# A hybrid decoder step on one core: one barrier per stage, first w_out slices and result rows split in the dilated stage, and a new order of the projection's first tiles and its last

## What is computed

```python
def _project(xn, pos, w_in, g_q_a, w_q_b, g_kv_a):
    z = xn @ w_in
    ...
    cq = _rmsnorm(z[..., :o1], g_q_a)
    q = (cq @ w_q_b).reshape(B, S, MLA_HEADS, MLA_NOPE + MLA_ROPE)
    ...
    ckv = _rmsnorm(z[..., o1:o2], g_kv_a)
    kr = _rope(z[..., o2:o3][:, :, None, :], pos)[:, :, 0, :]
    dq = _rope(z[..., o3:o3 + dw].reshape(B, S, DIL_HEADS, HEAD_DIM), pos)
    dk = _rope(z[..., o3 + dw:o3 + 2 * dw].reshape(B, S, DIL_HEADS, HEAD_DIM), pos)
    dv = z[..., o3 + 2 * dw:].reshape(B, S, DIL_HEADS, HEAD_DIM)
```

## Time and profile before

| | us |
|---|---|
| median of 3 runs | 1820.08 (1819.71 to 1823.69) |
| the profiled execution | 1819.3 |
| its span in the profile | 1817.7 |
| PE busy, share of the span | 1734.8, 95% |
| TensorE's mean granted clock, of full speed | 0.975 |

### The profile page before, as it was taken

One profiled execution on the slowest core, in us unless ns is written; L12 is line 12 of the kernel. 1 busy time (PEld: TensorE's weight loads), 2 busy tenths in 40 slices (PEclk: granted clock), 3 DMA queues, 4 the chain that ended last, 5 costly groups with the idle time before them and its releaser, 6 DMA issues.

```text
span 1817.7 us, 28003 instructions
## 1 busy us (share of the span) xinstructions
PE 1734.8 (95%) x9955; PEld 1511.8 (83%) x9955; DVE 860.7 (47%) x1802; ACT 660.8 (36%) x1329; POOL 573.3 (32%) x533
## 2 busy tenths in 40 slices
PE   7999979999997999999799999999999999999997
PEld 6788868888886888888688989888898898888985
DVE  6433325677775776766443332333423333333235
ACT  5222115666675666675322312111112121121113
POOL 0000003665561767778101312212112122131221
PEclk9999987999998999999899999999999999999999
DMA  8232133232326565655512668496585775956812
GB/s 283 96 105 102 67 106 101 54 102 63 85 61 162 164 179 160 179 159 180 193 50 49 132 144 136 114 164 118 118 161 120 152 115 129 161 110 133 150 43 103
DMA packets 156061, 227.44 MB, mean 125 GB/s; under 512 B 31063, under 2 KB 128984, under 8 KB 149528
## 3 DMA queue, kind: packets, MB, share of 16 engines
q1 hardware_dynamic: 153086, 159.39, 29.6%
q0 software_dynamic: 2880, 66.85, 22.1%
HBM read 201.12 MB, written 91.93 MB: 161 GB/s over the span
## 4 chain that ended last, share of the span: by engine, by line
PE 49%; DVE 1%; DMA 1%; ACT 0%; POOL 0%; issue 0%; ACTq 0%; DVEq 0%
PE wide L2476 22%; PE turn L2498 14%; PE rest L2477 7%; PE wide L2159 5%; DMA out_y_prompt<-f_gc 1%; PE wide L2574 1%; DVE o_wl L2139 1%; PE turn L2171 0%; DVE f_gc L2454 0%; ACT f_gc L2391 0%; PE rest L2483 0%; ACT f_rows L2398 0%; POOL f_st L2322 0%; PE rest L2507 0%; DVE f_al L2442 0%; DVE o_tl L2107 0%
## 5 line engine op out<-in xcount | busy, mean ns | idle before, releaser
L2411 DVE TENSOR_TENSOR acc<-turn,acc 128x512 f32<-128x512 f32 x198 | 136.5, 691 | 205.9 <-PE turn L2498 205.9
L2498 PE MATMUL turn<-f_dh,f_ah 128*128 128x512 f32 x396 | 157.8, 399 | 4.4 <-DVE f_al L2442 4.0
L2279 POOL TENSOR_TENSOR f_gl<-f_graw,f_gh 128x1024 fp32r<-128x1024 f32 x21 | 50.5, 2404 | 350.2 <-ACT f_gh L2329 350.2
L2498 PE MATMUL turn<-f_dl,f_ah 128*128 128x512 f32 x396 | 157.7, 398 | 0.0
L2498 PE MATMUL turn<-f_dh,f_al 128*128 128x512 f32 x396 | 157.6, 398 | 0.0
L990 POOL TENSOR_SCALAR a_pr<-a_pr,a_rden 128x256 f32<-128x256 f32 (+7 forms) x128 | 94.1, 747 | 187.7 <-DVE a_rden L1090 187.6
L2425 DVE SCALAR_TENSOR_TENSOR f_gc<-wide,f_coef,f_gc 128x832 f32<-128x832 f32 x44 | 47.7, 1084 | 209.4 <-ACT f_lasts L2349 206.5
L701 PE MATMUL zp<-win_h,xT_h 128*128 128x512 f32 (+1 forms) x288 | 112.7, 391 | 0.0
L701 PE MATMUL zp<-win_l,xT_h 128*128 128x512 f32 (+1 forms) x288 | 111.5, 387 | 0.0
L701 PE MATMUL zp<-win_h,xT_l 128*128 128x512 f32 (+1 forms) x288 | 111.5, 387 | 0.0
L1031 ACT ACTIVATE a_pr<-a_pr,a_nm 128x256 f32<-128x256 f32 (+7 forms) x128 | 98.6, 772 | 21.5 <-DVE a_nm L1084 20.8
(11 more groups left out here) (365 smaller groups left out, 4658.5 us busy)
## 6 DMA issues: line engine op xcount, KB each, us to landing
out_s_win_k<-in_state_win_k POOLq DMA_DIRECT2D x10, 3264.0 KB, 42.5
out_s_win_v<-in_state_win_v POOLq DMA_DIRECT2D x10, 3264.0 KB, 44.9
acc<-in_state_win_k SPq DMA_DIRECT2D x16, 768.0 KB, 6.0
acc<-in_state_win_v SPq DMA_DIRECT2D x16, 768.0 KB, 5.6
f_uraw<-in_w_up SPq DMA_DIRECT2D x22, 512.0 KB, 4.8
f_draw<-in_w_down SPq DMA_DIRECT2D x11, 1024.0 KB, 33.1
f_graw<-in_w_gate SPq DMA_DIRECT2D x21, 512.0 KB, 8.1
acc<-in_cache_kv_latent SPq DMA_DIRECT2D x128, 64.0 KB, 1.8
```

Of the source, the lines that this page charges most:

```text
L2279: nc.gpsimd.tensor_tensor(w_lo[n][:], w_raw[n][:], w_hi[n][:].bitcast(F32), ALU.subtract)\
L2411: nc.vector.tensor_tensor(a, dp[h][:], a, ALU.add).then_inc(S["d_add"], 1)
L2498: last = nc.tensor.matmul(dp[h][:], a[:, c, t * P:(t + 1) * P], w[:, c, h * 512:(h + 1) * 512], start=(c == 0 and j == 0), stop=(c == 1 an ...
```

## The change

**Barriers.** A class `Semaphores` takes the place of the clears: a stage's semaphores are cleared by POOL at the start of the next stage, and each stage has only its block's barrier. Semaphores that live across a stage are kept to the end. SP no longer waits at the end of the attention for its last stores: the waits are in the output stage, on SP behind the x loads, and on ACT before slice 7 of w_out.

**Early slices.** Three tiles of 2 x 1024 columns (`io["lead"]`) serve first as buffers of the window side. At the end of the dilated stage slices 0 and 1 of w_out are split into them (lead_hi on ACT, lead_lo on POOL), and row tile 0 (lead_rows on ACT and DVE). Later they are buffers of the MLP. On DVE the merge of the last sample (a_qn) is moved ahead of one copy to a_ot. ACT and DVE split only slices 2 to 7 in the output stage. For tile 0 PE takes both column halves of a slice in a row. x rows 0 and 1 are loaded without a wait, x rows 2 to 7 behind the sixth of the low slices, row tile 2 without a wait. Split of tile 1 is ahead of the gate slice on ACT, and a fill of the padding rows goes from DVE's lead to the end of tile 0.

**Project.** In the first two tiles group 2 of t1 comes ahead of the latent transposes of t1, t0's group 3 ahead of t1's query, and t1's group 3 ahead of its key_value; ACT, DVE and SP follow. In the last tile (the samples) group 3 comes ahead of the query, and the latent keys and values, which nobody reads for the samples, are not computed (6 matmuls and two copies).

```diff
             store_dq(t0)
             store_dk(t0)
             turns_in(t0)
+            store_dv(t0)
             store_dq(t1)
             store_q(t1)
-            store_dv(t0)
             store_dk(t1)
             turns_in(t1)
+            store_dv(t1)
             store_kv(t1)
-            store_dv(t1)
             with sp.Fori(0, 2) as it:
...
-                key_turned(t)
-                query(t)
-                sliding_value(t)
-                key_value(t)
+                if samples(t):
+                    sliding_value(t)
+                    query(t)
+                else:
+                    key_turned(t)
+                    query(t)
+                    sliding_value(t)
+                    key_value(t)
...
                 key_value(t0)
                 latent_hi(t1)
                 key_turned(t1)
+                sliding_value(t0)
                 query(t1)
-                sliding_value(t0)
                 prep(Step.of(2))
                 square(Step.of(3))
+                sliding_value(t1)
                 key_value(t1)
-                sliding_value(t1)
 
             walk(act, prep, main, lead)
...
-                query(t)
-                group(t, 3)
-                key_value(t)
+                if samples(t):
+                    group(t, 3)
+                    query(t)
+                else:
+                    query(t)
+                    group(t, 3)
+                    key_value(t)
 
             def lead():
...
                 group(t0, 2)
+                group(t1, 2)
                 latent(t1)
-                group(t1, 2)
+                group(t0, 3)
                 query(t1)
-                group(t0, 3)
                 prep(Step.of(2))
+                group(t1, 3)
                 key_value(t1)
-                group(t1, 3)
...
     def sync_end(self, sp):
-        if self.events is self.stages[1]:
-            for f in range(2):
-                sp.wait_ge(self.S[f"o_out{f}"], 16 * 2 * PAIRS)
...
-    "vector": {(0, "out"): -2, (1, "k_turn"): 1, (1, "score"): 1},
+    "vector": {(1, "lead_rows"): -3, (0, "out"): -2, (1, "k_turn"): 1, (1, "score"): 1},
...
+        elif e[0] == "lead_lo":
+            i = e[1]
+            wh, rows, wl = self.io["lead"]
+            pool.wait_ge(self.io["lead_hi"], i + 1)
+            nc.gpsimd.tensor_tensor(wl[:, i, :], self.io["acc"][:, i, :], wh[:, i, :].bitcast(F32), ALU.subtract)\
+                .then_inc(self.io["lead_lo"], 1)
 
     def scalar(self, act, e):
         S, R, nc = self.S, self.ring.S, self.nc
...
+        if e[0] == "lead_hi":
+            i = e[1]
+            act.wait_ge(self.io["w_ahead"][0], 16)
+            act.wait_ge(S["o_ps"], 3 * DEC_B - 1)
+            nc.scalar.copy(self.io["lead"][0][:, i, :], self.io["acc"][:, i, :]).then_inc(self.io["lead_hi"], 1)
+        elif e[0] == "lead_rows":
+            act.wait_ge(self.io["o_ahead"], 16)
+            act.wait_ge(S["o_ps"], 3 * DEC_B)
+            nc.scalar.copy(self.io["lead"][1][:, 0, :], self.io["acc"][:, PT, :]).then_inc(self.io["lead_hi"], 1)
         bank = self.ring.ready(act, e) if self.bank_use(e) else None
...
-        if e[0] == "pre":
+        if e[0] == "lead_rows":
+            rows = self.io["lead"][1]
+            dve.wait_ge(self.io["lead_hi"], 3)
+            nc.vector.tensor_tensor(rows[:, 1, :], self.io["acc"][:, PT, :], rows[:, 0, :].bitcast(F32), ALU.subtract)\
+                .then_inc(self.io["lead_lo"], 1)
+        elif e[0] == "pre":
...
             x = io["x_prompt"].rearrange("(t p) d -> p t d", p=P)
-            sp.wait_ge(S["w_lo"], 2)
             sp.dma_start(acc[:, 0:2, :], x[:, 0:2]).then_inc(S["x_in"], 16)
-            sp.wait_ge(S["w_lo"], KC)
+            sp.wait_ge(S["w_lo"], KC - 2)
             sp.dma_start(acc[:, 2:PT, :], x[:, 2:PT]).then_inc(S["x_more"], 16)
             ahead["sync_split"](sp)
             sp.dma_start(acc[0:NS, PT, :], io["x_sample"]).then_inc(S["x_last"], 16)
+            for done, n in io["stored"]:
+                sp.wait_ge(done, n)
             with sp.Fori(2, PT) as n:
...
             def lead():
-                split(Step.of(0))
-                for k in range(KC):
+                for k in range(2, KC):
                     act.wait_ge(io["w_ahead"][k // 2], 16)
-                    nc.scalar.copy(wh[:, k, :], acc[:, k, :]).then_inc(S["w_hi"], 1)
+                    if k == KC - 1:
+                        for done, n in io["stored"]:
+                            act.wait_ge(done, n)
+                    nc.scalar.copy(wh[k], acc[:, k, :]).then_inc(S["w_hi"], 1)
+                split(Step.of(1))
                 ahead["scalar"](act)
-                split(Step.of(1))
...
         def tensor(pe):
             def prep(t):
-                pe.wait_ge(S["t_lo"], t.n + 1)
+                if t.first:
+                    pe.wait_ge(io["lead_lo"], 3)
+                else:
+                    pe.wait_ge(S["t_lo"], t.n)
                 if not t.first and not t.second:
 
                     pe.wait_ge(S["h_ok"], t.n - 1)
-                for c in range(2):
+                halves, slices = range(2), range(KC)
+                for c, k in ([(c, k) for k in slices for c in halves] if t.first else [(c, k) for c in halves for k in slices]):
                     cols = slice(c * 512, c * 512 + 512)
-                    for k in range(KC):
-                        if t.first and c == 0:
-                            pe.wait_ge(S["w_lo"], k + 1)
-                        for i, (a, b) in enumerate(((oT_h, wh), (oT_h, wl), (oT_l, wh))):
-                            last = nc.tensor.matmul(mp[t.odd][:, cols], a[t.odd][:, k, :], b[:, k, cols],
-                                                    start=(k == 0 and i == 0), stop=(k == KC - 1 and i == 2))
+                    if t.first and c == 0 and k > 1:
+                        pe.wait_ge(S["w_lo"], k - 1)
+                    for i, (a, b) in enumerate(((oT_h, wh), (oT_h, wl), (oT_l, wh))):
+                        last = nc.tensor.matmul(mp[t.odd][:, cols], a[t.odd][:, k, :], b[k][:, cols],
+                                                start=(k == 0 and i == 0), stop=(k == KC - 1 and i == 2))
...
+            pool.wait_ge(O["t_lo"], 1)
...
+            io["sems"].clear()
...
+    def clear(self):
+        for n in ranges([s.num for s in self.groups[-2][1]]):
+            self.nc.gpsimd.sem_clear(n)
+
+    def close(self):
+        if len(self.groups) > 1:
+            self.groups.pop(0)[0].close()
...
         for phase in PHASES:
-            if phase is attention:
-                io["acc"] = ctx.enter_context(nc.sbuf_tensor("acc", [P, NT, D_MODEL], F32))
-                io["w_ahead"] = [ctx.enter_context(nc.semaphore(f"w_ahead{i}")) for i in range(4)]
-                io["o_ahead"] = ctx.enter_context(nc.semaphore("o_ahead"))
-            with ExitStack() as own:
-                used = []
-
-                def sem(name):
-                    used.append(own.enter_context(nc.semaphore(name)))
-                    return used[-1]
-
-                phase(nc, sem, io)
-
-                for n in ranges([s.num for s in used]):
-                    nc.gpsimd.sem_clear(n)
-                nc.all_engine_barrier()
-
-
+            sems.open()
+            phase(nc, sems.sem, io)
+            sems.close()
```

101 lines of the change are left out of this document (69 added, 32 removed).

## The result

Over eight runs of each, side by side, the changed kernel takes 1804.36 us (1800.69 to 1813.02) and the kernel before 1822.03 (1819.71 to 1823.78): ratio 0.9911, 95% interval 0.9894 to 0.9927. By the ratio that is 16 us (17.7 between the medians), not 9.6. Its profiled execution took 1801.88, span 1800.3, against 1819.3 and 1817.7: 17.4 less of span.

The account below looks back on a forecast made before the run. PE was busy 95% of the span, so only its waits or half clock could be won. Gains 0.8 + 1.3 + 7.6 - 0.1 = 9.6 us gave 1809.7 profiled, 1810.5 for the median; range 1806.5 to 1815.5.

Parts of the forecast that it names:

- The MLP reuses the early buffers, with its waits behind the last output tile: 0: MLP, under other edits: reusing the early slices' buffers there was costed at 0 us.
- Output boundary, the opening: Dilated to output stage: opens at about 876.2, 2.7 us earlier; PE waits 1.1 us in place of 7.4.
- Early slices and rows: End of the dilated stage: work moved ahead of the boundary costs 0, at most 1 us; margin 0.3.
- rival (2): Rows arrive late at the output boundary, or the project gap stays as long: sum 6.0 to 7.0, 1813.5 us, chance 0.12.
- Tile 0: Output stage: PE is never short of slices, so tile 0 ends at 887.2, 9.4 us earlier.
- Tile 2: Output stage: PE waits 1.2 to 2.0 us, taken as 1.7, for row tile 2's load, queued behind 3 MB of x rows.
- The clock: Output stage: a half-clock stretch or the stall for tile 2 takes 1.8 us, leaving 7.6 of 9.4.
- rival (1): Output stage: second loss of clock after a stall of some 2 us for tile 2; boundary 5.8, 1812.3 us, chance 0.22.
- Project stage: First tiles gain 0.8 us (gap 3.6 in place of 4.1, half clock takes 2.2); last tile gains 1.3.
- The range: Whole kernel: 1806.5 to 1815.5 us, from the better case to the second loss of clock.
- (4): Output stage: tile 2's load slower, with the 3 MB taking 26 us; stall 16.3, time 1825.0 us, chance 0.05.

Follow-up runs that it names:

- e7: Changed kernel with fillers placing the lead tiles and f_ah, f_al all at 128 modulo 256, as o_wh and o_wl; 1803.45 us, ratio to before 0.9916.
- e6: Kernel before, with a 160-byte filler ahead of f_ah and f_al, giving them the place of w_down's halves modulo 256; 1810.43 us, ratio 0.9951.
- e12: Changed kernel with the waits for the last stores at the attention's end and a second barrier at two phase boundaries put back; 1806.57 us, ratio to before 0.9933.
- e4: Changed kernel with 32-byte fillers for both the lead tiles and f_ah, f_al, so all start at multiples of 64 bytes; 1810.23 us, ratio to before 0.9939.
- e8: e7 with the rows of the input weights' high half (win_h) also padded from 7808 to 7936 bytes; 1802.2 us, ratio to before 0.9902.
- e11: Changed kernel with output row tile 0 in the old order, all eight slices for the left column half, then the right; 1806.76 us, ratio to before 0.9938.
- e9: e8 with row tile 2 loaded ahead of the 3 MB of x rows and tile 0's rows ahead of w_out's last two loads; 1795.64 us, ratio to before 0.9870.
- e3: Changed kernel with a 32-byte filler beside the lead tiles only, so they start at a multiple of 64 bytes; 1809.78 us, ratio to before 0.9942.
- e10: Changed kernel with every project stage edit taken back (tile orders, six unused matmuls, stores' order); 1806.34 us, ratio to before 0.9928.
- e5: Separate kernel of matmuls only, varying the operands' byte offsets; 48 matmuls took 10.96 us at distance 0 modulo 256, 11.20 to 11.29 elsewhere, 11.05 with moving 64 ahead.

## Why the prediction was wrong, point by point

**The failed step** is "The MLP reuses the early buffers, with its waits behind the last output tile: 0". The waits were looked at, the place was not. The term measured -7.8 us in the MLP (0.80 in each of ten passes). The same reuse has a counterpart in the output projection, where 0.23 a matmul was carried over from before: +1.3 in tiles 3 to 8 and about 0.7 in tiles 0 to 2 (0.4 in tiles 0 and 1 against e7, 0.3 in tile 2 as in the other even tiles). e6 shows the MLP's term alone in the kernel before: 25.29 to 24.49, ratio 0.9951.

**Output boundary, the opening: right.** Forecast 1.1 us from the last a_o matmul to the first of the output stage, measured 1.22, and e12 shows what the old way costs here: 3.1.

**Early slices and rows: right, with the rival in it.** Costed at 0 with 1 as its bound and a margin of 0.3: the margin was 0.3 in the changed kernel's profile, and 1 us was paid in e4, e7, e8 and e11. This was rival (2), in four of the profiles of the changed order.

**Tile 0: right.** No wait on o_wl; tiles 0 and 1 took 22.28 from the opening to the transposes against the forecast 22.0; in e7, with the operands placed alike, 21.89. e11 shows that the order of the halves carries it: without it tile 0 takes 14.4 in place of 11.2.

**Tile 2: size right, and the cause not refuted.** A wait of 1.2 to 2.0 was forecast, 1.48 was measured. It was put down to the 3 MB alone. The chain names the gate slice as well: it took 8.07 us to land where it took 6.8 before, and POOL's split of it holds SP. Whether that cost anything isn't shown. The 3 MB were issued at 880.35; with the 10.9 us that they took before they landed at 891.3 (an estimate, the trace has no landing for them), and tile 2 was cast 3.4 later, where 2.9 was forecast. Tile 2 was usable 8.8 us after its issue at 885.87, and 4.3 us where it went ahead of the 3 MB (e9). The Trainium skill, "DMA: Bandwidth & Descriptors", section "Queues, rings and completion order", has descriptors consumed in ring order; the two traces agree with it.

**The clock: the sum came out, the case was another.** 1.8 were set aside for a lost clock or a stall; here the stall was paid and the clock held. In e4, e7 and e8 (waits of 2.6, 3.0 and 2.2) it was lost after the stall, rival (1); in e3 and e10 (1.97 and 2.19) it held. Forecast for tiles 0 to 2 was 7.6, measured 6.86, and the missing 0.7 is what the placement took there.

**Project stage: right in sum, wrong in its halves.** Forecast 0.8 + 1.3 = 2.1, measured 1.73 in this pair and 2.3 on the means. The gap in the first tiles (timeline) was 3.29, not 3.6:

```profile
55.06 0.80 PE L706 MATMUL zp<-win_h,xT_h 128*128 128x512 f32 x1 [3.29 <-DVE dqk L577]
```

SP's queue at the end of the stage, to set beside the earlier trace rows:

```profile
251.34 2.64 SPq L274 DMA_DIRECT2D out_s_win_v<-dvm  x8
254.81 0.48 SPq L274 DMA_DIRECT2D scratch_s_q<-qm  x1
257.96 0.43 SPq L969 DMA_DIRECT2D a_qn<-scratch_s_q  x1
```

The query's store is issued at 254.81 and the first load at 257.96. The forecasts, 255.1 and 257.9, leave out what the first tiles give. That was 0.3 in this pair: the transposes of one and the same input tile start at 99.28 against 99.60. So the first load, 1.4 earlier than before, has 1.1 from the last tile (forecast 1.3). The step that was off is the half clock behind the gap. PE was as far at 55.06 as before at 58.17, 3.1 earlier (forecast 3.0), but its matmuls ran at half clock until 60.8, which took back 2.8 in place of 2.2.

**The attention: not in the sum, and it was luck.** 2.25 of the 17.4 lie in the two stages of attention, where only a clear, the last events and the place of three window buffers are new. The windows of the changed kernel:

```profile
270.00:287.00 17.00, 15.57 (x71) 13.39 (x72) 8.08 (x22) 9.13 (x28) 4.54 (x8) 0.52 0.23 55
287.00:298.00 11.00, 8.96 (x60) 7.75 (x60) 6.34 (x23) 6.00 (x17) 2.58 (x5) 1.00 0.21 48
```

and the second stretch before:

```profile
287.00:298.00 11.00, 9.03 (x33) 7.24 (x32) 4.36 (x14) 4.80 (x13) 2.51 (x4) 0.54 0.20 50
```

Before, PE ran at half clock until 297, after until 286. Which short waits cost the clock differs from profile to profile of nearly the same code. Added up over the attention, the half clock lasted 61 us before and 51 after, 38 in e11 with the shortest attention (606.6) and 69 in e10 with the longest (615.8). That the earlier start is what moved it is not shown. Over the twelve kernels the attention took 606.6 to 615.8; the mean of the four with the old project stage is 611.8, of the eight others 610.0. Whether the difference of the means is more than chance the runs don't settle. The scatter of the changed kernel's eight runs also goes with the clock: its mean is 0.979 to 0.982 in the five up to 1804.66 and 0.973 to 0.976 in the three from 1808.41 on.

**The range.** It had bounds for waits, transfers and the clock, and none for the pace of the matmuls themselves. With the 7.8 of the MLP 1810.5 would have been 1802.7, and with the placement's loss in the output stage (1.3 and 0.7) 1804.7. That this is near 1804.36 is in part chance, since the attention's 2.25 isn't in it. Two figures of the rivals don't follow from their own terms, and change nothing: in (2), 9.6 less 1 to 2 for the rows is 7.6 to 8.6, less the 0.8 of the first tiles 6.8 to 7.8, not 6.0 to 7.0; in (4), the 11.4 are used up at 896.8 + 11.4 = 908.2, not 907.5.

## What to carry to other kernels

When an edit moves a tile that TensorE reads, work out its byte offset, and that of its partner, modulo 256, and then measure: a filler of 160 bytes decides here over 0.2342 or 0.2268 us a matmul in the down projection, where TensorE is the bound, while the up product and the input projection did not follow the rule. Count the start of the columns in the offset too, which e8 left out. Where a wait is removed, look at what the next operand's load is queued behind, and send the small one that is wanted first ahead of the big one (e9, with two such loads: 5.3 us at the boundary). And where a kernel's clock depends on waits of 1 to 3 us, read each experiment by stretches of its profile, since its total can move by more than the edit.

## What the runs showed of the hardware

- TensorE's spacing of fp32r matmuls of 512 columns, each with its own weights, depends on the distance between moving and stationary operand in SBUF: 0.2283 us at a multiple of 256 bytes, 0.2302 with the moving one 64 ahead, 0.2333 to 0.2352 at every other multiple of 32 (e5, all else idle, granted clock 1.0). The down projection follows it (0.2268 to 0.2342), the up product does not (0.50 us for its three matmuls at distance 0 and at 160). The Trainium skill, "SBUF — State Buffer", section "SBUF: two separate sides", says that TensorE never waits for another engine's accesses; that is not contradicted, for here nothing else ran: it is TensorE's two reads that differ, and no run shows why.
- The clock: ahead of tile 2 waits of 1.97 and 2.19 us kept it (e3, e10), waits of 2.23 to 3.05 lost it (e4, e7, e8); at the boundary 1.22 to 2.43 kept it and 3.30 lost it (e12). The length alone doesn't decide: the wait of the earlier trace rows is 1.73 to 1.76 us in all twelve profiles, and it was followed by a stretch at half clock in five of them and not in seven.
- A barrier of all engines costs 0.4 us from the last arrival to the first issue (871.91 to 872.32, changed kernel); with a second one and a store's landing in front it is 2.5 (e12).
